# Hybrid MLA and mLSTM trunk in split fp32: value banks and q's diagonal emptied on ScalarE, an early exponential, a bank of its own for the second head's q

## The reference, cut to what matters

```python
proj = u @ w_in                                   # 1024 -> 512 + 256 + 32
c_q  = proj[..., :512]
c_kv = proj[..., 512:768]
k_r  = proj[..., 768:]
q  = (rms_norm(c_q, g_q) @ w_uq)                  # 16 heads of 64 + 32
kv = (rms_norm(c_kv, g_kv) @ w_ukv)               # 16 heads of 64 (k) + 64 (v)
s  = (q_n . k_n + rope(q_r) . rope(k_r)) * scale, masked
o  = softmax(s) @ v                               # in blocks of 128 queries
h  = h + o @ w_o
```

## Time and profile before

| | |
|---|---|
| median of 3 runs | 1231.27 us (1229.65 to 1232.26) |
| profiled execution | 1231.35 us, its span 1229.5 us, so 1.85 us lie around the span |
| PE busy | 1201.9 us, 98% of the span |
| DVE, ACT, POOL busy | 601.2, 447.5 and 269.5 us (49%, 36%, 22%) |
| granted TensorE clock, mean of the span | 0.994 |
| chain of work that ended last | PE 80% of the span, waiting for nothing shown ("issue") 1%, DVE 1%, ACT 0% |
| page part 2, busy tenths of PE in 40 slices of 30.7 us | 7 9 8, then 9 until the last, which is 6 |

### The profile page before, as it was taken

One profiled execution on the slowest core, in us unless ns is written; L12 is line 12 of the kernel. 1 busy time (PEld: TensorE's weight loads), 2 busy tenths in 40 slices (PEclk: granted clock), 3 DMA queues, 4 the chain that ended last, 5 costly groups with the idle time before them and its releaser, 6 DMA issues.

```text
span 1229.5 us, 15577 instructions
## 1 busy us (share of the span) xinstructions
PE 1201.9 (98%) x6054; PEld 1012.5 (82%) x6054; DVE 601.2 (49%) x824; ACT 447.5 (36%) x707; POOL 269.5 (22%) x283
## 2 busy tenths in 40 slices
PE   7989999999999999999999999999999999999996
PEld 6768888888888888888879899987888888888885
DVE  5776666444334334344357545655443443433431
ACT  5447777532212222122344255534221221221242
POOL 2232343322102002012212145532210210200211
PEclk9999999999999999999999999999999999999998
DMA  6211112233332333322233424412333232333211
GB/s 186 52 29 30 29 29 76 69 103 103 103 103 69 104 102 102 102 80 92 75 99 104 146 91 101 110 35 73 99 103 103 89 100 87 101 102 102 82 56 69
DMA packets 117353, 107.29 MB, mean 87 GB/s; under 512 B 21318, under 2 KB 115620, under 8 KB 117292
## 3 DMA queue, kind: packets, MB, share of 16 engines
q1 hardware_dynamic: 117260, 106.43, 28.4%
q10 hardware_dynamic: 32, 0.01, 0.0%
HBM read 104.32 MB, written 2.11 MB: 87 GB/s over the span
## 4 chain that ended last, share of the span: by engine, by line
PE 80%; issue 1%; DVE 1%; ACT 0%; POOL 0%; POOLq 0%; DVEq 0%; ACTq 0%
PE ps L1490 25%; PE ps L1492 24%; PE ps L1491 24%; PE ps L1898 1%; PE ps L1900 1%; PE ps L1899 1%; PE ps L1927 0%; PE ps L1929 0%; PE ps L1928 0%; PE ps L1773 0%; PE ps L1775 0%; PE ps L1774 0%; PE ps L1910 0%; PE ps L1533 0%; PE ps L1522 0%
## 5 line engine op out<-in xcount | busy, mean ns | idle before, releaser
L1053 DVE TENSOR_TENSOR wlo<-raw,whi 128x2048 fp32r<-128x2048 f32 (+3 forms) x90 | 196.8, 2190 | 158.0 <-ACT whi L715 158.0
L715 ACT CAST whi<-raw 128x2048 fp32r<-128x2048 f32 (+3 forms) x149 | 184.8, 1269 | 238.9 <-PE ps L1492 234.8
L1490 PE MATMUL ps<-xl,whi 128*128 128x512 f32 (+1 forms) x624 | 245.1, 393 | 0.2 <-issue 0.2
L1491 PE MATMUL ps<-xh,whi 128*128 128x512 f32 (+1 forms) x624 | 242.9, 389 | 0.0
L1492 PE MATMUL ps<-xh,wlo 128*128 128x512 f32 (+1 forms) x624 | 242.9, 389 | 0.0
L1490 PE MATMUL ps<-ul,whi 128*128 128x512 f32 x592 | 231.8, 392 | 2.6 <-DVE wlo L1053 2.6
L1492 PE MATMUL ps<-uh,wlo 128*128 128x512 f32 x592 | 230.9, 390 | 0.0
L1491 PE MATMUL ps<-uh,whi 128*128 128x512 f32 x592 | 230.8, 390 | 0.0
L627 POOL TENSOR_TENSOR ul<-sq,uh 128x512 fp32r<-128x512 f32 x64 | 83.7, 1309 | 521.1 <-ACT uh L915 521.1
L1272 DVE TENSOR_TENSOR h<-ps,h 128x512 f32<-128x512 f32 x80 | 55.0, 690 | 193.9 <-PE ps L1492 190.3
L1490 PEld LDWEIGHTS ps<-xl,whi 128*128 128x128 f32 (+1 forms) x624 | 116.6, 187 | 26.6 <-issue 2.2
(11 more groups left out here) (252 smaller groups left out, 1626.7 us busy)
## 6 DMA issues: line engine op xcount, KB each, us to landing
raw<-in_mlp_w SPq DMA_DIRECT2D x64, 1024.0 KB, 5.4
raw<-in_mlstm_w_in SPq DMA_DIRECT2D x12, 1024.0 KB, 5.3
raw<-in_mla_w_o SPq DMA_DIRECT2D x4, 1024.0 KB, 5.1
raw<-in_mlstm_w_o SPq DMA_DIRECT2D x4, 1024.0 KB, 5.4
raw<-in_mla_w_in SPq DMA_DIRECT2D x3, 1024.0 KB, 5.4
raw<-in_mla_w_uq SPq DMA_DIRECT2D x16, 192.0 KB, 2.5
x_tok<-in_x SPq DMA_DIRECT2D x4, 512.0 KB, 7.7
mx<-m_rows SPq DMA_DIRECT2D x8, 256.0 KB, 3.9
```

The lines of the kernel that those rows point to most:

```text
L715: last = sc.copy(hi, src)
L1053: last = v.tensor_tensor(lo, src, hi.bitcast(F32), ALU.subtract)
L1490: mm(o, ah, bl, start=first, stop=False)
L1491: mm(o, ah, bh, start=False, stop=False)
```

## The change

- ScalarE takes over the value banks 2 to 7 (`v_evac`) and the diagonal of c_q's norm (four activations with a scale, instead of `stat_diag`). VectorE keeps value banks 0 and 1 and only makes `var` (`stat_var`).
- ScalarE runs one exponential of 128x1 into `rsum[:, 0:1]` ahead of the diagonal. The exponentials of the heads behind it then have no ACT_TABLE_LOAD of their own.
- ScalarE's order: diagonal, banks 2, 3, 4, two parts of c_q, bank 5, two parts of c_q, banks 6 and 7, the strip of head 1 (ahead of k instead of behind it), k, q of head 0, the strip of head 2, q of head 1 (the strip stood behind it).
- VectorE's order: the multiplication of part m + 1 of c_q stands ahead of the low part m, where the value copies stood.
- GpSimd makes `pick` ahead of the sums of c_q's norm instead of behind its power.
- q of head 1 goes to bank 6 (`B_PT + 1`) instead of bank 0, and TensorE waits for `q_tab` only from head 2 on.

TensorE's instructions and their order stay as they are. The core of the diff:

```diff
+        def q_bank(head):
+            return B_PT + 1 if head == 1 else B_Q
...
@@ GpSimd
+            (pick's waits and its instruction, moved here)
             norm_adds(NORM_CQ)
             norm_pow(NORM_CQ)
@@ ScalarE
-            c_high(0, ckv, ckvh, G_KV, 2)
+            c_high(0, ckv, ckvh, G_KV, range(2))
...
-            c_high(2, cq, cqh, G_Q, 4)
+            def v_evac(t):
+                act.wait_ge(gemm_done, T_VA + t + 1)
+                sc.copy(v_part(t), bank((T_VA + t) % RING).rearrange("p (m n) -> p m n", n=P)).then_inc(gemm_evac, 1)
+
+            sc.activation(rsum[:, 0:1], ones[:, 0:1], ACT.Exp)
+            act.wait_ge(rcol_ready, NORM_CQ + 1)
+            act.wait_ge(stat_bc, NORM_CQ)
+            for t in range(TT):
+                last = sc.activation(diag[:, 0, P * t:P * t + P], ident[:], ACT.Copy, scale=rcol[:, t:t + 1])
+            last.then_inc(diag_ready, 1)
+            act.wait_ge(gemm_evac, T_VA + 2)
+            for t in (2, 3, 4):
+                v_evac(t)
+            c_high(2, cq, cqh, G_Q, range(0, 2))
+            v_evac(5)
+            c_high(2, cq, cqh, G_Q, range(2, 4))
+            v_evac(6)
+            v_evac(7)
+            split(N_PAIR + 1, "q")
             for e in range(2):
                 k_high(e, 0)
-            split(N_PAIR + 1, "q")
             q_high(0)
+            split(N_PAIR + 2, "kq")
             q_high(1)
-            split(N_PAIR + 2, "kq")
@@ VectorE
             for t in range(2):
                 v_evac(t)
-            stat_diag(NORM_CQ, QRANK)
-            for t in range(2, 5):
-                v_evac(t)
+            stat_var(NORM_CQ, QRANK)
...
             stat_row(NORM_CQ, r_b)
-            for m in range(4):
-                v.tensor_tensor(cq[:, m, :], cq[:, m, :], r_b[:], ALU.mult).then_inc(c_norm, 1)
+            v.tensor_tensor(cq[:, 0, :], cq[:, 0, :], r_b[:], ALU.mult).then_inc(c_norm, 1)
             for m in range(4):
                 if m < 3:
-                    v_evac(5 + m)
+                    v.tensor_tensor(cq[:, m + 1, :], cq[:, m + 1, :], r_b[:], ALU.mult).then_inc(c_norm, 1)
                 dve.wait_ge(c_hi, 2 + m + 1)
...
-                v.tensor_tensor(qtmp[:], bank(B_Q), tab[:], ALU.mult).then_inc(q_tab, 1)
+                v.tensor_tensor(qtmp[:], bank(q_bank(head)), tab[:], ALU.mult).then_inc(q_tab, 1)
@@ TensorE, q_half
-                    if head:
+                    if head >= 2:
                         pe.wait_ge(q_tab, head)
```

More of the change, by code:

```diff
@@ L207, in trunk, with v_part @@
         v_all = nc.alloc_sbuf_tensor_at("v_all", [P, PAIRS, S], F32, offset=uh_at)
+        def v_part(t):
+            half, tt = t // TT, t % TT
+            return v_all[:, 4 * half:4 * half + 4, P * tt:P * tt + P]
         def v_slot(i):
@@ L591, in _ @@
             norm_pow(NORM_KV)
+            spot = [ident[0:16, 8 * part:8 * part + 8].rearrange("r (e b) -> r b e", e=2).unsqueeze(3)
+                    .broadcast_to([16, TT, 2, VD]) for part in range(2)]
+            pool.wait_ge(trig_ready, 2)
+            pool.wait_ge(kr_new, 1)
+            g.tensor_tensor(pick[:, :, :].rearrange("r b (e n) -> r b e n", e=2), spot[0], spot[1], ALU.add) \
+                .then_inc(pick_ready, 1)
             norm_adds(NORM_CQ)
@@ L605, in _ @@
             pool.wait_ge(wlo_ready, N_PAIR)
[L606 to L611, removed]
             for head in range(3):
@@ L764, in c_high @@
             def c_high(n_before, src, hi, gain, tiles):
-                for m in range(tiles):
+                for m in tiles:
                     act.wait_ge(c_norm, n_before + m + 1)
@@ L1069, in par_columns, with stat_var @@
                 dve.wait_ge(par_ready, n)
-            def stat_diag(norm, width, sums=None):
+            def stat_var(norm, width, sums=None):
                 dve.wait_ge(stat_col, norm + 1)
@@ L1075, in stat_diag @@
                     .then_inc(var_ready, 1)
+            def stat_diag(norm, width, sums=None):
+                stat_var(norm, width, sums)
                 dve.wait_ge(rcol_ready, norm + 1)
@@ L1158, in v_evac @@
             def v_evac(t):
-                half, tt = t // TT, t % TT
                 dve.wait_ge(gemm_done, T_VA + t + 1)
-                v.tensor_copy(v_all[:, 4 * half:4 * half + 4, P * tt:P * tt + P],
-                              bank((T_VA + t) % RING).rearrange("p (m n) -> p m n", n=P)).then_inc(gemm_evac, 1)
+                v.tensor_copy(v_part(t), bank((T_VA + t) % RING).rearrange("p (m n) -> p m n", n=P)).then_inc(gemm_evac, 1)
             for t in range(2):
                 v_evac(t)
-            stat_diag(NORM_CQ, QRANK)
-            for t in range(2, 5):
-                v_evac(t)
+            stat_var(NORM_CQ, QRANK)
             for e in range(2):
@@ L1614, in q_half @@
                     ah, al, bh, bl = pq(whi[s])[:, k, :], pq(wlo[s])[:, k, :], cqh[:, k, :], cql[:, k, :]
-                    mm(bank(B_Q), ah, bl, start=(k == 0), stop=False)
-                    mm(bank(B_Q), ah, bh, start=False, stop=False)
-                    last = mm(bank(B_Q), al, bh, start=False, stop=(k == 3))
+                    mm(bank(q_bank(head)), ah, bl, start=(k == 0), stop=False)
+                    mm(bank(q_bank(head)), ah, bh, start=False, stop=False)
+                    last = mm(bank(q_bank(head)), al, bh, start=False, stop=(k == 3))
                 if half:
```

## The result

| | before | after |
|---|---|---|
| median | 1230.74 us of 6 runs (1229.55 to 1232.26) | 1223.32 us of 6 runs (1221.94 to 1223.71) |
| ratio, on the same chip | | 0.9938 [0.9925, 0.9951] |
| profiled execution, its span | 1231.35, 1229.5 us | 1223.51, 1221.5 us |

The change makes the kernel 7.4 us faster by the medians. The interval of the ratio is 6.0 to 9.2 us of 1230.74, so the 6.2 us that were forecast lie at its near end. The forecast was 1225.1 us, from 1223.2 to 1227.7.

What follows compares the result with a forecast made beforehand. TensorE was taken as bound by its waits, 5.9 us within 21 us, plus a lowered clock behind the longest. Fourth scores 4.7 us earlier plus 1.5 from the clock made 6.2, so 1225.1 us, range 1223.2 to 1227.7.

Steps and rivals of the forecast that it cites:

- the stretch: TensorE from the first value tile's start to head 2's second half-query; forecast 6.2 us shorter, from 33.06 us before.
- From 88.81 on TensorE works without a wait: After the matmul starting at 88.81 us, everything follows TensorE, so time gained by then is kept to the end.
- Diagonal: c_q's norm: ScalarE writes the diagonal earlier, so TensorE's spread starts at 63.95 instead of 64.47 us, 0.5 us gained.
- Value bank: Before k: ScalarE copies bank 5 in time, TensorE's 1.65 us wait goes, and k starts 1.8 us earlier still.
- Bank of its own, strip's new wait: Before head 1's q: the 1.14 us wait for q_tab goes; its strip comes 0.55 us late, bounds 0 and 1.1.
- First exponential: Before head 0's exponential: early table load takes 1.30 us off the path; fourth scores at 79.95 against 84.68, 4.7 us earlier.
- Clock: Behind the fourth scores: with the longest gap cut from 2.72 to 1.7 us, full clock gives back 1.5 us.
- The clock falls again: Rival: gaps of 0.55 and 1.7 us still lower TensorE's clock, giving 1226.6 us; chance 0.14.
- ScalarE's list late by a link: Rival: ScalarE's chain of diagonal, bank 5 and strip runs late, 1226.8 us, or 1228.3 with clock loss; chance 0.12.
- The banks don't do what they say: Rival: c_q's chain, not bank 5, held k; its 1.8 us return as another wait, 1226.9 us; chance 0.06.
- ScalarE blocked as VectorE was: Rival: fourteen ScalarE instructions stretched; gain gone at 0.7 us each, 1235.7 us at 1.0 each; chance 0.02.
- Better, 1224.0: Case: no strip gap (0.55), more from clock (0.2), no held `q_low` (0.15), rest 0.2; chance 0.04.

Runs made afterwards that it cites:

- before_again: The kernel before, unedited, run and traced once more: 1231.66 us, ratio 1.0005.
- after_again: The changed kernel, unedited, run and traced once more: 1223.38 us, ratio 0.9942 to the kernel before.
- both_dve: Changed kernel with both the diagonal of c_q's norm and value banks 2 to 7 back on VectorE: 1226.54 us, ratio 0.9955 to the kernel before.
- one_bank: Changed kernel with q of head 1 in bank 0 again, behind the wait for q_tab: 1225.37 us, ratio 0.9948 to the kernel before.
- late_exp: Changed kernel without the early exponential of 128x1: 1226.84 us, ratio 0.9962 to the kernel before.
- exp_only: Kernel before with only the early exponential added: 1230.52 us, ratio 1.0000.
- banks_dve: Changed kernel with value banks 2 to 7 copied by VectorE again: 1223.1 us, ratio 0.9934 to the kernel before.
- diag_dve: Changed kernel with the diagonal of c_q's norm written by VectorE again: 1223.26 us, ratio 0.9932 to the kernel before.
- max_first: Changed kernel with the first three row maxima and first exponential ahead of head 1's q low part and rounding: 1223.17 us; repeated, 1222.18 us.
- strip_first: Changed kernel with ScalarE rounding head 1's strip ahead of value banks 6 and 7: 1225.74 us, ratio 0.9953 to the kernel before.

## Where the prediction held, and which step failed

Inside the stretch the mechanism and the sum held: 6.32 us measured for 6.2 forecast. The step that failed is the one that closes the sum, "From 88.81 on TensorE works without a wait", by which all that lies outside the stretch was put at nothing. The kernel became 7.4 us faster and not 6.2, and of the missing 1.2 us the stretch accounts for 0.1. TensorE's list of waits for the kernel before, from which the forecast read only the three of rows 1, has these as well, besides two for the first loads (3.9 and 3.5 us):

```profile
PE ps L1490 <- DVE wlo L1053: 2.6, 1, 2.6
...
PE ps L1522 <- ACT sq L729: 1.1, 1, 1.1
PE ps L1645 <- DVE xl L1058: 0.9, 1, 0.9
```

The first is longer than two of the three that were read. It ends at 839.83 us, and TensorE's clock can fall behind it. The two pairs of traces of the unedited kernels show where the gain lies:

| us gained | first pair | second pair (`before_again`, `after_again`) |
|---|---|---|
| before the first value tile | 0.97 | 0.36 |
| the stretch | 6.32 | 6.32 |
| from there to the last norm's power | -0.13 | 1.37 |
| behind it, where the output is written | 0.85 | 0.49 |
| profiled spans | 8.0 | 8.5 |

The stretch repeats to 0.01 us, and the other three terms don't. The bullets take the forecast's terms in their order.

- **Diagonal (0.5 us).** The spread starts 0.53 us earlier. The power was held to 1.52 us, still in time. That ScalarE had to do it was not so: without `pick` beside it, VectorE's was in time too. So `pick`, which stands among the terms at nothing, is the part that removes this wait.
- **Value bank (1.8 us).** k gained 2.45 us against the first value tile, of which 0.53 are from the spread, so 1.9. The cause was given too narrowly. Taking the diagonal or the banks off VectorE is each enough; both back costs 1.8 us (`both_dve`), and there the wait stands before head 0's q and hardly before k (13.49 instead of 13.25).
- **Low parts of c_q (no wait).** The changed kernel has none.
- **Bank of its own, strip's new wait (1.14 leave, 0.55 come).** The wait is 0.67 us, within 0 to 1.1. The bank's worth of 1.0 us is shown by `one_bank`.
- **First exponential.** The fourth scores start at 24.19 from the first value tile, against 24.20 forecast. That it fits to 0.01 is in part luck: head 1's q was 0.17 us later than forecast, and the way from there to the fourth scores 0.18 shorter, of which 0.15 are the hold of `q_low` that didn't come (GpSimd lost 0.5 us off the path instead). The forecast's own positions give a gap of 1.5 us, not the 1.7 that it states; measured are 1.35. And the sentence that the table takes 1.30 us from the path is wrong for the changed order: with the strip's rounding moved ahead, the load would have hidden but for 0.36 us (`late_exp`), and in the kernel before the early exponential alone brought the scores 1.30 us forward but moved no time (`exp_only`). The sum was right since it followed the chain and didn't add the 1.30.
- **Table switch by the page.** The early load's row is 1.28 us and the next instruction starts 0.02 behind it. The drain of 1.38 us that the Trainium skill, "ScalarE: Activation LUTs", "What ACT_TABLE_LOAD costs", adds is not there; the row decides, and the 1223.8 us by the page were reached for other reasons.
- **Clock (1.5 us).** Within the stretch it holds: from the fourth scores to its end it is 4.13 us before and 2.55 after, 1.58 given back. But it was sized from one place only. Behind the wait of 2.63 us near 836 us, which is in every trace, the clock fell alike in the first pair (granted clock 0.58 over 839 to 843 us before, 0.57 over 834 to 838 after), and stayed at 1.00 in `after_again`, `banks_dve`, `diag_dve` and `max_first`. That is the 1.37 us of the second pair.
- **Start and output (nothing).** The first value tile starts at 54.74 us (`max_first`) to 55.99 (`before_again`), at 54.78 and 55.63 in the two traces of the changed kernel. From the last norm's power to the end it is 9.64 and 9.63 us in the two of before, 8.79 and 9.14 in the two of the changed kernel, and up to 10.00 in the others (`both_dve`). The forecast took the clock's scatter as the first rival only, in the direction of a loss, and the range's lower end had nothing in it for a gain outside the stretch.
- **What stays open.** The 1.2 us over the forecast can be a lasting effect or these executions' share of start, 836 us and output. The two comparisons give 7.6 and 7.1 us (0.9938 and 0.9942 of 1230.74), with 1.6 to either side, which 6.3 us would fit too. The mean granted clock of a run's span, 0.995 to 0.997 in all 11 runs of the changed kernel and 0.991 to 0.995 in those of before, decides little: the fall in the stretch alone, 1.7 us of clock in 1229.5, is 0.0014 of it and counted already. Three traces with the order of before have their first value tile at 55.90 on average and eleven with the changed order at 55.20; no run looked for a cause of that.
- **Rivals.** *The clock falls again*: it didn't in either trace of the changed kernel, but it did in `late_exp` and `strip_first`, whose gap is only 0.36 and 0.41 us longer, so this rival was near. *ScalarE's list late by a link*: it takes 1.28 us for the diagonal and 0.57 to 0.59 for a copy, so no. *The banks don't do what they say*: k has no wait in the changed kernel; the rival's picture shows in `both_dve` alone. *ScalarE blocked as VectorE was*: it wasn't stretched beside GpSimd, against the 0.7 us each from which this decides. (ScalarE's slack there was summed wrongly: the work of 1.5 + 3.3 + 2.6 + 0.8 us leaves 2.9 of the 11.1 us and not 3.5, which gives 0.65 us each and about 1236.3 us at 1.0.) *Better, 1224.0*: of its parts `q_low` wasn't held (0.15) and the clock gave 0.08 more than 1.5, but the strip's wait came and was longer. The time was reached outside the stretch.

## What to carry to other kernels

Follow the bound engine's list of waits as one chain and count positions from a point that the change can't touch; gains that are added part by part count redundant moves twice (diagonal and banks here) and credit a hidden operation with its full length (the table load). Before a wait is taken out, see what the next longer one behind it does: here one of 0.67 us less made the gap behind it 0.41 longer, the clock fell, and the stretch became 0.8 us longer. A term for the clock should be given as a spread over executions, and its good side belongs in the range too. And the whole list of the bound engine's waits belongs in the forecast, those outside the place that is changed as well: what they cost can differ between two executions of the same kernel by more than a part of the change is worth.

## What the runs showed that was not expected

- A few tenths of a microsecond can go with a fall of the clock. In these traces it fell behind gaps of 1.71, 1.76 and 2.72 us before the fourth scores and behind 1.44 followed by 0.81, and stayed at full behind 1.35 to 1.37 there and behind 1.65 and 1.66 further ahead. Since 2.63 us near 836 us left it at full in some traces, the length of the gap alone doesn't decide; what else does was not tested.
- Where VectorE and GpSimd meet, which of them loses depends on when: VectorE's four writes took 0.87 one norm earlier, 2.29 beside a strip's low part and 3.30 beside `pick` and that strip; the low part of head 2's strip and `q_low` together cost GpSimd 0.5 us in the changed kernel, but both engines lost (2.70 and 1.12 us instead of 2.26 and 0.69) when `q_low` came 0.77 us earlier (`strip_first`).
- The load of a table didn't wait for what its activation waits for: it ran at 77.91 us, 0.02 behind the instruction before it, and hid in the wait but for 0.36 us (`late_exp`).
- In the first 14 us of the kernel before, the granted clock's column reads 1.00 while matmuls start 0.43 us apart; only the distance of starts tells that TensorE is slow there.
